# One inference step of a small hybrid decoder: the second mixer's pooling and its products put behind its convolution, layer-1 memory rows turned earlier

## What is computed

```python
def odd_mixer(h, ...):
    u, ga, gb = split(h @ w_in, [512, 1024])
    # pooling half: means over windows of 2, 4, 8, 16 positions, one window for each 128 channels
    pooled = concat([(csum_end - csum_start) / count for w in (2, 4, 8, 16)]) - u
    pooled = einsum('blgc,gcd->blgd', pooled, pool_w) * pool_scale
    # convolution half: 31 taps for each channel, then a norm over the 512 channels
    c = causal_dwconv(ga * sigmoid(gb), cw, cb)
    mu, var = mean(c), mean(square(c - mu))
    c = silu((c - mu) * rsqrt(var + EPS) * cng + cnb)
    return concat([pooled, c]) @ w_out

def mem_kv(mem, g, wk, wv):
    m = rmsnorm(mem, g)
    return m @ wk, m @ wv
```

## Time and profile before

| | us |
|---|---|
| median of 3 runs | 1556.95 |
| lowest and highest run | 1556.41 and 1562.45 |
| the profiled execution, its own time | 1560.83 |
| its span, first to last instruction | 1558.9 |

### The profile page before, as it was taken

How to read it: one execution, slowest core, us unless ns; L and a number is a source line. 1 busy time by engine, 2 the same in 40 slices (tenths; PEclk the granted TensorE clock), 3 DMA queues, 4 the chain that set the end, 5 groups by cost and what they waited for, 6 DMA issues and landing times.

```text
span 1558.9 us, 22150 instructions
## 1 busy us (share of the span) xinstructions
PE 1447.7 (93%) x9354; PEld 1003.0 (64%) x9354; DVE 469.1 (30%) x1300; ACT 206.3 (13%) x430; POOL 126.1 (8%) x156
## 2 busy tenths in 40 slices
PE   7999999999998999999997899849999999999991
PEld 5887677788776888878886776634444444444440
DVE  3345656520352211141397336120000000000003
ACT  2121112101211100000112221120000000000001
POOL 3003414300010200000000001020000000000001
PEclk9998889999998999999999998879999999999996
DMA  9743644645483994434443358736999999999962
GB/s 280 220 149 95 167 105 146 234 151 173 147 324 134 335 388 154 142 108 156 155 142 119 125 192 299 264 137 245 385 396 380 387 402 356 373 391 352 399 245 94
DMA packets 184056, 368.26 MB, mean 236 GB/s; under 512 B 8419, under 2 KB 117243, under 8 KB 183808
## 3 DMA queue, kind: packets, MB, share of 16 engines
q1 hardware_dynamic: 162600, 292.47, 52.7%
q0 software_dynamic: 19264, 71.23, 13.2%
q10 hardware_dynamic: 2096, 3.15, 0.6%
HBM read 339.13 MB, written 28.49 MB: 236 GB/s over the span
## 4 chain that ended last, share of the span: by engine, by line
PE 87%; DVE 7%; DMA 3%; issue 2%; POOL 1%; ACT 1%; SPq 0%; ACTq 0%; POOLq 0%; DVEq 0%
PE psum L886 32%; PE psum L1426 13%; PE psum L1298 10%; PE psum L1432 6%; PE psum L1465 6%; PE psum L1195 5%; PE psum L1471 3%; DVE arena L2198 2%; DMA ring<-in_cache_mem_v_dram 1%; PE psum L1237 1%; PE psum L1262 1%; PE psum L1229 1%; PE psum L911 1%; DMA expert_rows<-arena 1%; PE psum L1443 1%
## 5 line engine op out<-in xcount | busy, mean ns | idle before, releaser
L886 PE MATMUL psum<-hT,ring 128*128 128x264 f32 x1168 | 276.2, 399 | 1.1 <-ACT hT L1508 1.1
L886 PEld LDWEIGHTS psum<-hT,ring 128*128 128x128 f32 x1168 | 228.1, 196 | 49.1 <-issue 6.9
L886 PE MATMUL psum<-arena,ring 128*128 128x264 f32 x992 | 229.2, 395 | 9.3 <-ACT arena L1669 5.0
L886 PEld LDWEIGHTS psum<-arena,ring 128*128 128x128 f32 x992 | 192.9, 195 | 44.1 <-ACT arena L1669 5.4
L1298 PE MATMUL psum<-hT,ring 128*128 128x264 f32 x704 | 157.0, 386 | 0.0
L1298 PEld LDWEIGHTS psum<-hT,ring 128*128 128x128 f32 x704 | 133.8, 190 | 22.9
L1426 PE MATMUL psum<-ring,arena 128*64 128x384 f32 (+1 forms) x704 | 137.2, 541 | 0.0
L1195 PE MATMUL psum<-ring,arena 128*128 128x256 f32 x512 | 115.9, 388 | 0.0
L1195 PEld LDWEIGHTS psum<-ring,arena 128*128 128x128 f32 x512 | 99.2, 195 | 19.3 <-issue 5.3
L1791 DVE TENSOR_TENSOR arena<-psum,rstd 128x264 f32<-128x264 f32 (+3 forms) x117 | 43.8, 393 | 214.4 <-PE psum L1298 118.8
L1426 PEld LDWEIGHTS psum<-ring,arena 128*64 128x64 f32 x704 | 49.1, 137 | 79.9 <-issue 79.9
(11 more groups left out here) (432 smaller groups left out, 1227.4 us busy)
## 6 DMA issues: line engine op xcount, KB each, us to landing
ring<-in_moe_w_dram SPq DMA_DIRECT2D x72, 1024.0 KB, 17.2
arena<-in_moe_w_dram SPq DMA_DIRECT2D x40, 1024.0 KB, 15.0
ring<-in_moe_w_dram SPq DMA_DIRECT2D x44, 768.0 KB, 16.3
ring<-in_ffn_w_dram SPq DMA_DIRECT2D x30, 1024.0 KB, 5.4
ring<-in_w_in_even_dram SPq DMA_DIRECT2D x22, 1024.0 KB, 5.9
ring<-in_cache_mem_k_dram POOLq DMA_DIRECT2D x16, 1024.0 KB, 8.2
ring<-in_cache_mem_v_dram POOLq DMA_DIRECT2D x16, 1024.0 KB, 6.4
arena<-in_moe_w_dram SPq DMA_DIRECT2D x20, 768.0 KB, 17.3
```

The costliest lines, as they stand in the source:

```text
L886: ins = mm(outs_[m][0:mw, 0:T], wv[:, k, m * mw:(m + 1) * mw], rhs(base + k), start=(base + k == 0), stop=(kc == len(chunks) - 1 and k == ...
```

## The change

In `psum_groups`, and in the lists of PE, ACT and DVE alike:

- `memory_rows(1)` runs inside the loop over the SwiGLU blocks, after the tiles of block b = 7 of 0 to 10, on PE and DVE. The wait for `hid_ready` stands behind the `ost` transposes, directly ahead of `f2`.
- On PE, tails and `pw` go behind `var`; ahead of them run two parts of `xv1`, `mu`, two parts of `xv1`, `var`. `wout1` no longer waits for all four SiLU tiles ahead of its first matmul: the function `mixed` waits for tile k - 3 of `conv_act` ahead of each matmul with k = 4 to 7 of its 8, and the first four read the pooled half.
- On ACT, values and the root of the variance go ahead of tails and `pw`.
- On DVE, `sample_taps` and the taps go ahead of the poolings. Two poolings (windows 2 and 4) run between the taps and the subtraction of `mu`, two (8 and 16) between the squares and the reciprocal. Their instructions are the same.

```diff
@@ psum_groups @@
     for b in range(FF // SLOT_N):
         g += [("f1", 2 * b), ("f1", 2 * b + 1)] + ([("ss", FFN_NORM[0])] if b == 0 else []) + [("f3", 2 * b), ("f3", 2 * b + 1)]
-    g += memory_rows(1)
+        if b == 7:
+            g += memory_rows(1)
...
-    g += lin_ss("win1", 12, ODD_NORM) + mem_k(1) + [("tail1",), ("tail2",)] + [("pw", i) for i in range(4)]
-    g += v1[:2] + [("mu",)] + v1[2:4] + [("var",)]
+    g += lin_ss("win1", 12, ODD_NORM) + mem_k(1) + v1[:2] + [("mu",)] + v1[2:4] + [("var",)]
+    g += [("tail1",), ("tail2",)] + [("pw", i) for i in range(4)]
@@ tensor engine @@
-            memory_rows(1)
-            pe.wait_ge(sem("hid_ready"), 1)
-
+                if b == 7:
+                    memory_rows(1)
...
+            pe.wait_ge(sem("hid_ready"), 1)
             linear("f2", 4, [8, 8, 6], lambda k: hid[:, k, :], memory=1)
...
             memory_k(1)
+            tokmajor("xv1", range(2))
+            pe.wait_ge(sem("conv_taps"), OT * (CK - 1))
+            sumsq(("mu",), lambda k: mixo[:, OT + k, :], OT, T)
+            tokmajor("xv1", range(2, 4))
+            pe.wait_ge(sem("csq_ready"), 1)
+            sumsq(("var",), lambda k: csq[:, k, :], OT, T)
             pe.wait_ge(sem("tail1_ready"), 1)
...
-            pe.wait_ge(sem("conv_act"), 4)
             for g in range(OT):
                 taken(pe, ("pw", g))
-            linear("wout1", 4, [8], lambda k: mixo[:, k, :])
+
+            def mixed(k):
+
+                if k >= OT:
+                    pe.wait_ge(sem("conv_act"), k - OT + 1)
+                return mixo[:, k, :]
+
+            linear("wout1", 4, [8], mixed)
@@ scalar engine @@
             memory_k(1)
+            memory_out("xv1", Vt, range(4))
+            full(act, ("var",))
+            free(("var",), af(rstd[:], bank(("var",))[:, 0:T], ACT.Sqrt, scale=1.0 / 512, bias=eps[:, 0:1]))
             for key, dst, n in ((("tail1",), tok1, 23), (("tail2",), tok2, 38)):
...
-            memory_out("xv1", Vt, range(4))
-            full(act, ("var",))
-            free(("var",), af(rstd[:], bank(("var",))[:, 0:T], ACT.Sqrt, scale=1.0 / 512, bias=eps[:, 0:1]))
@@ vector engine @@
+                if b == 7:
+                    memory_rows(1)
             dve.sem_inc(sem("hid_ready"), 1)
-            memory_rows(1)
...
+            for t in (2, 3):
+                sample_taps(t)
+            some_taps(4 * CK, range(OT))
+            dve.wait_ge(sem("conv_taps"), OT * (CK - 1))
             n_up = PST + NP
-            for g, win in enumerate(WINDOWS):
+
+            def pooling(g):
+
+                win = WINDOWS[g]
...
-            for t in (2, 3):
-                sample_taps(t)
-            some_taps(4 * CK, range(OT))
-            dve.wait_ge(sem("conv_taps"), OT * (CK - 1))
+
+            pooling(0)
+            pooling(1)
             full(dve, ("mu",))
...
             v.tensor_tensor(csq[:, :, :], mixo[:, OT:, :], mixo[:, OT:, :], ALU.mult).then_inc(sem("csq_ready"), 1)
+            pooling(2)
+            pooling(3)
             taken(dve, ("var",))
```

## The result

The changed kernel takes 1541.28 us (median of 4 runs, 1539.98 to 1542.72); the kernel before, run beside it, 1558.49 (1556.41 to 1562.45). The ratio is 0.9884, 95% interval 0.9865 to 0.9903: faster by 1.2%, some 18 us by the ratio (15.1 to 21.0 by its interval) and 17.2 by the medians. The profiled execution took 1542.72 with a span of 1540.2, so the span fell by 18.7 us.

A forecast was written before the change was run, and what follows sets the result against it. PE, 87% of the chain, bounds the kernel, with 15.84 us idle and 5.67 slow clock to win. 5.5 + 14.2 = 19.7 us off 1560.83 gives 1541.1; that execution lay 3.88 above the median, so 1537.3, range 1531 to 1545.

The forecast's parts named there:

- The bound and the three stalls: PE holds 87% of the chain; it idles 3.63 us ahead of `f2`, 7.20 ahead of `mu`, 5.01 ahead of `wout1`.
- the layout: Second mixer's new order timed step by step in the old trace's clock: `wout1` ends at 878.14 instead of 892.33.
- Memory rows amid the SwiGLU: Moving the rows into the SwiGLU removes 3.63 us idle and 1.87 slow clock at `f2`: gain 5.5 us.
- Rival 2: DVE's burst on the memory rows holds PE in the SwiGLU: 1542.8 us, at the far bound 1547.1; chance 0.05.
- the bound of 9.8: Memory rows in the SwiGLU: most they could cost, DVE's whole burst on the path, 9.8 us; 0 was charged.
- The second mixer: From the keys to `wout1`, the new order gains 14.2 us: 16.0 idle and clock, less 1.67 waits and 0.15 overlap.
- the signs named for a right forecast: Among them: no PE wait above 1 us from keys to `wout1`, `mu` near 1.95, about 1.7 us of small waits.
- The table load: On ACT ahead of SiLU in the second mixer: charged 1.28 us, without the Trainium skill page's about 1380 ns of drain.
- The sum: Whole kernel: 5.5 + 14.2 = 19.7 us, 1541.1 against the profiled execution, 1537.3 as the forecast median.
- rival 3: The next stage waits for its cache loads and takes back the mixer's 14.2 us: 1551.5, no change; chance 0.07.
- rival 4: Slower: the clock falls in the mixer and all 128 `wout1` records run at 1.2 GHz, 1565.9 us; chance 0.03.
- rival 1: PE's clock falls after `var`: one slow `wout1` start, 1.86 us, gives 1539.2, two such stretches 1541.0; chance 0.10.

The follow-up runs named there:

- ost_first: The kernel before with the old-state transposes put ahead of the memory rows on PE and DVE, both still behind the SwiGLU: 1559.5 us, one run.
- silu_all: The changed kernel with one wait for all four SiLU tiles ahead of `wout1`: 1549.22 us, one run.
- rows_only: The kernel before with only the memory rows moved into block 7 and the `hid_ready` wait behind the old states: 1554.9 against 1560.23 us, ratio 0.9963.
- mixer_only: The changed kernel with the memory-row and `hid_ready` edits taken back, only the mixer's new order left: 1546.9 against 1560.23 us, ratio 0.9909.
- rows_block10: The changed kernel with the memory rows after the SwiGLU's last block, 10, instead of block 7: 1549.16 us, one run.

## Why the prediction was right

**The bound and the three stalls.** Right. That a bank, not `hid_ready`, held `f2` is shown by `ost_first`; that it was the second of the two is read from the times alone (the third `mT` copy ended 0.11 us ahead of `f2`). The wait ahead of `wout1` comes back in `silu_all`. The wait for the taps ahead of `mu` stays in `rows_only` and goes in `mixer_only`, with all edits of the mixer at once; that DVE's new order removed it is the bracket's and the layout's argument, and no kernel tried it apart.

**Memory rows amid the SwiGLU.** Forecast 5.5, measured 5.4 in the stretch. Rival 2 is out: the 192 records behind the rows took 42.89 us, 0.2234 each, the full-clock price, so the burst held PE nowhere in the SwiGLU. With the burst uncovered `rows_block10` lost 9.5 us, near the bound of 9.8, but not by the burst alone: 7.49 of it are idle time and 1.86 the clock (21.71 for 19.85), so the nearness is in part luck.

**The second mixer.** Forecast 14.2, measured 13.9. The layout held step by step: margin ahead of `mu` 0.35 to the end of `xv1` (822.58 + 7.07 - 829.30), as forecast, and 0.19 to the start of `mu`, whose first record overlaps that end; `mu` 1.94 (1.95), wait for the last pooling 1.12 (0.73), wait for the last `pw` eviction 0.83 (0.68), and 28.78 for `wout1` (28.56 and 0.26 of waits). The first two waits were undersized by 0.5 us, and the third was nearly right. PE came to the first of them 0.5 us sooner than laid out (841.01 - 822.58 = 18.43 from `xv1` to the end of the tails, 18.91 forecast), since in the trace each group starts ahead of the modelled end of the one before. So `wout1` ended only 0.25 us late, 51.18 for 50.93. ACT's last eviction ended on time, 842.84 + 1.82 - 822.58 = 22.08 for 22.11, and `wout1` started 0.32 behind it, for which nothing was charged. Of the signs named for a right forecast, one failed by this: a PE wait above 1 us, the 1.12 ahead of `pw`; and the small waits are 2.2 us, not 1.7.

**The table load.** The charge of 1.28 us held. ACT's timeline in the changed kernel:

```profile
842.84 1.82 ACT L1673 ACTIVATE arena<-psum,par 128x264 f32<-128x264 f32 x4 [1.17 <-PE psum L1334]
844.68 1.28 ACT L1676 ACT_TABLE_LOAD   x1
845.98 2.10 ACT L1676 ACTIVATE arena<-arena,par 128x264 f32<-128x264 f32 x4
```

The load began 0.02 us after the last eviction ended, and SiLU 0.02 us after the load. DVE's four scalings were done by 845.35, so SiLU had nothing else to wait for that could hide a rest. The Trainium skill, page ScalarE: Activation LUTs, section What ACT_TABLE_LOAD costs, has 1283 ns and some 1380 ns of drain: the first is what the trace shows; the second doesn't appear here, and the measurement decides.

**The sum.** The two stretches give 19.3 us; the span fell by 18.7. The rest isn't the change's: the old-state transposes started 0.77 us later than in the trace before, and the SwiGLU, up to which the code is the same, already started 0.77 later (the kernel before, then the changed one):

```profile
509.61 7.28 PE L1298 MATMUL psum<-hT,ring 128*128 128x264 f32 x32
510.38 7.28 PE L1299 MATMUL psum<-hT,ring 128*128 128x264 f32 x32
```

19.3 less 0.77 is 18.6; at the start of the expert stage 18.1 are there (under 17 was named as a sign of being wrong), at the end 18.7, so the stages between lost 0.4 and the expert stage won 0.6. So the gain came through nearly whole and rival 3 is out; rival 4 and rival 1 are out by the windows at 1.00.

**The forecast time.** 1537.3 was 4.0 us too low. The weak step is the last of the sum: carrying the result from the profiled execution to the median of three runs. Against the profiled execution the sum had given 1541.1; it took 1542.72, and the median was 1541.28. The kernel before has since given medians of 1558.49 (4 runs, the three among them), 1560.23 (13) and 1562.14 (7): 1556.95 was at the low side of its spread. Beside 1558.49 that is 1.5 of the 4.0 us. The other 2.5 are 19.7 against 17.2 by the medians; since the interval of the gain, 15.1 to 21.0, holds both, the runs can't tell them apart. The 19.7 us themselves were over by 0.4 in the stretches.

## What to carry to other kernels

Where PE holds the chain, look for its brackets and at the clock behind each one; a wait of several us cost its own length here and 1.5 to 3.2 us of slow clock behind it, and reordering what the vector engine does first removed both without removing any work. Work that another engine must do in a burst belongs where that engine has slack and where no bank or signal of it is asked for until the burst ends: here three blocks ahead of the end, and 9.5 us lost if only at the end. Ask first for what PE really waits: where it is a bank, exchanging two groups in the order of banks won 4.4 of the 5.4 us here. A wait for a whole group, put ahead of a loop, is worth splitting by element: here 5.2 us for the wait on four tiles, and 1.3 more for two others.

## What was not expected of the hardware

The price of a slow clock after an idle time isn't fixed. The same 5.01 us ahead of `wout1` cost 1.86 us in the kernel before (30.42 for 28.56) and 3.23 in `rows_only` (31.79); `mu` behind 7.2 us took 3.89 and 3.44 in the same two. Why is open. Every idle time of 3.63 us and more in the stretches shown was followed by records wholly or partly at half clock (windows of 0.50 to 0.62 where shown); none of 1.12 us or less was, and products thrown away in the wait kept the full clock.
